# First two weight tiles of the dense part prepared inside the S5 output stage of a two-block layer kernel

## The chip, the cores and the metric

The kernel runs on one core of a Trainium2 chip. The metric is the device time of one execution in microseconds (us); lower is better. The engines are named as the profile names them: PE is the matrix engine (PEld its weight loads), DVE the vector engine, ACT the scalar engine, POOL the GpSimd engine, and SP the sync engine, which here only issues DMAs. A suffix q (SPq, PEq) means the sequencer of that engine.

## The reference, cut to what matters

One sequence of 2048 tokens by 1024 features goes through two blocks. The first block is a state-space mixer (S5) with a gated linear unit, a squared-ReLU feed-forward part and a gated per-layer embedding; the second has attention, an mLSTM and a convolution branch. The change touches the seam between the S5 mixer and everything behind it:

```python
y = (einsum('blgp,ghp->blgh', xs_re, c_re) - einsum('blgp,ghp->blgh', xs_im, c_im))
y = gelu(y.reshape(bsz, seqlen, D_MODEL) + d_skip * uf)      # S5 output
a, g = jnp.split(y @ w_glu, 2, axis=-1)                      # first weights of the dense part
mix = a * jax.nn.sigmoid(g)
x = x + mix
x = x + sqrelu_mlp(rmsnorm(x, norm_ffn), mlp_w1, mlp_w2)
```

Products are in float32 accuracy. The kernel gets that from three passes on a faster number format: each operand is split in a high part (a cast) and a low part (operand minus high part), and high x high, high x low and low x high are added up.

## The kernel before, in words

The program is a sequence of stages, each a `Block` in which every engine has its own instruction list; between two stages all engines meet at a barrier. The stages that matter here:

- `s5_states` (ends at about 214 us of the span): the scan over chunks.
- `s5_outputs` (214.5 to 332.7 us): eight rounds q = 0 to 7. In a round PE forms the S5 outputs of four pairs (L616 to L624), ACT applies the GELU (L653), PE turns the result (transposes, L635), ACT casts the first half of the tokens to the high part `AHL[:, 0, q]` (L660), DVE forms the low part `AHL[:, 1, q]` (L677) and copies the second half of the tokens to `later` (L681), and SP stores that to memory (L600, `y_hi`). PE and ACT turn and copy round q-1 behind the outputs of round q. SP also loads the matrices `s5_mt` of round q+2 (L442, eight DMAs of 128 KB for each round, each of many small pieces), in the same instruction list and so behind its wait for round q-1's store. DVE forms the matrices `ca` (L453 to L461). POOL has nothing to do in this stage.
- `dense` (from 332.7 us on): all the matrix products of the layer with streamed weights, for two halves of the tokens (`NB` = 2, `TB` = 1024). The weights are 124 tiles of 128 x 1024 floats, `wall`. Tile w goes through slot s = w % 2: SP loads it to `WR[s]` (`load`, L872, 512 KB), ACT casts it to `WH[s]` (`hi`, L910), POOL forms `WL[s]` (`lo`, L1129) and so frees `WR[s]` (semaphore `raw_free`), and PE multiplies (`product`, L1417). SP's order at the stage's start: `gains`, `w_gi`, four small vectors, tiles 0 and 1, tiles 2 and 3 (each behind `raw_free`), then `X`. ACT's order: the cast of `gwr` (L916), then tiles 0 and 1. POOL's order: `ones` (L1121), `gwl` (L1125), then tiles 0 and 1. PE starts on tile 0 when `raw_free` has reached 3, that is when `WL[0]` is there.

The steps of the prediction name: `s5_outputs` with its sync, scalar, vector and tensor programs; `s5_stage`, which opens the buffers; and in `dense` the first lines of the sync, scalar and gpsimd programs.

Of the kernel before, what the change touches and what calls it, by code (L numbers as in the profile page):

```python
# [11 lines left out]
P = 128  # L12
# [558 lines left out]
def s5_outputs(nc, env, d, ctx):  # L571

    sb, ps, sem = tools(nc, ctx)
    U, AHL, xs, ident = env["U"], env["AHL"], env["xs"], env["ident"]

    mt = [env["mt0"], sb("s5_mt1", [P, 2 * QP, T * H])]
    ca = [env["ca0"], sb("s5_ca1", [P, 2, QP, T, H])]
    yc = sb("s5_yc", [P, 2, T, P])
    later = sb("s5_later", [P, 2, SEQ // 2])
    by_step = lambda v: v.rearrange("p (c t) -> p t c", t=T)  # L580
    psy = [ps(f"s5_psy{i}", [P, 2, T * H]) for i in range(4)]
    psq = [ps(f"s5_psq{i}", [P, 4, NCH]) for i in range(4)]
    ld_m = [sem("s5_ld_m0"), sem("s5_ld_m1")]
    feed, fed = sem("s5_feed2"), sem("s5_fed2")
    y_mm, gelu_done, y_turned, hi_done, lo_done = (sem("s5_" + x) for x in ("y_mm", "gelu_done", "y_turned", "hi_done", "lo_done"))
    st_y = [sem("s5_st_y0"), sem("s5_st_y1")]
    with nc.Block() as block:
        @block.sync
        def _(sp):
            def load(q):  # L590
                if q >= 2:
                    sp.wait_ge(y_mm, 2 * (q - 1))
                s5_load(sp, d, q, mt[q % 2], ld_m[q % 2])

            load(1)
            for q in range(NQ):
                if q + 2 < NQ:
                    load(q + 2)
                sp.wait_ge(lo_done, 4 * (q + 1))
                sp.dma_start(d["y_hi"][q, :, SEQ // 2:], later[:, q % 2]).then_inc(st_y[q % 2], 16)  # L600
            for i in range(2):
                sp.wait_ge(st_y[i], 16 * (NQ // 2))

        @block.tensor
        def _(pe):
            def outputs(q):
                if q:
                    pe.wait_ge(ld_m[q % 2], 16 * S8 * ((q + 1) // 2))
                for pr in range(2):
                    if q:  # L610
                        pe.wait_ge(gelu_done, 4 * (q - 1) + 2 * pr + 2)
                    for jj in (2 * pr, 2 * pr + 1):
                        j = q * QP + jj
                        for g in range(2):
                            o, m = psy[2 * pr + g][:, jj % 2], mt[q % 2][:, 2 * jj + g]
                            pe.matmul(o, U[:, 0, 2 * j + g], m, start=True, stop=False)  # L616
                            pe.matmul(o[:, T * H // 2:], U[:, 1, 2 * j + g], m[:, 0:T * H // 2], start=False, stop=False)

                        if q:
                            pe.wait_ge(fed, q)  # L620
                        for ri in range(2):
                            for g in range(2):
                                rows = slice(g * 64, (g + 1) * 64)
                                last = pe.matmul(psy[2 * pr + g][:, jj % 2], xs[rows, ri, j, 0:NCH],  # L624
                                                 ca[q % 2][rows, ri, jj].rearrange("p t h -> p (t h)"),
                                                 start=False, stop=(ri == 1))
                    last.then_inc(y_mm, 1)

            def turn(q):
                pe.wait_ge(gelu_done, 4 * (q + 1))  # L630
                for i in range(4):
                    if q:
                        pe.wait_ge(lo_done, 4 * (q - 1) + i + 1)
                    for t in range(4):
                        last = pe.transpose(psq[i][:, t], yc[:, q % 2, 4 * i + t], ident[:])  # L635
                    last.then_inc(y_turned, 1)

            for q in range(NQ + 1):
                if q < NQ:
                    outputs(q)  # L640
                if q:
                    turn(q - 1)

        @block.scalar
        def _(act):
            for q in range(NQ + 1):
                if q < NQ:
                    for pr in range(2):
                        act.wait_ge(y_mm, 2 * q + pr + 1)
                        if q >= 2:  # L650
                            act.wait_ge(y_turned, 4 * (q - 1))
                        for g in range(2):
                            act.activation(yc[:, q % 2].rearrange("p t (j g h) -> p j g t h", h=H, g=2)[:, 2 * pr:2 * pr + 2, g],  # L653
                                           psy[2 * pr + g][:].rearrange("p j (t h) -> p j t h", h=H),
                                           ACT.Gelu_apprx_tanh).then_inc(gelu_done, 1)
                if q:
                    r = q - 1
                    for i in range(4):
                        act.wait_ge(y_turned, 4 * r + i + 1)
                        act.copy(by_step(AHL[:, 0, r])[:, 4 * i:4 * i + 4], psq[i][:, :, 0:NCH // 2]).then_inc(hi_done, 1)  # L660

        @block.vector
        def _(dve):
            def feedout(q):
                if q >= 2:
                    dve.wait_ge(y_mm, 2 * (q - 1))
                s5_feedout(dve, env, q, ca[q % 2], env["cat"], feed, N_FEED * (q - 1)).then_inc(fed, 1)
                dve.wait_ge(fed, q)

            feedout(1)  # L670
            for q in range(NQ):
                if q + 2 < NQ:
                    feedout(q + 2)
                for i in range(4):
                    dve.wait_ge(hi_done, 4 * q + i + 1)
                    steps = slice(4 * i, 4 * i + 4)
                    dve.tensor_tensor(by_step(AHL[:, 1, q])[:, steps], psq[i][:, :, 0:NCH // 2],  # L677
                                      by_step(AHL[:, 0, q])[:, steps].bitcast(F32), ALU.subtract)
                    if q >= 2:
                        dve.wait_ge(st_y[q % 2], 16 * (q // 2))  # L680
                    dve.tensor_copy(by_step(later[:, q % 2])[:, steps], psq[i][:, :, NCH // 2:]).then_inc(lo_done, 1)  # L681
# [20 lines left out]
def s5_stage(nc, env, d):  # L702
    with ExitStack() as stage:
# [6 lines left out]
        with ExitStack() as win:  # L710
            env["Win"] = win.enter_context(nc.sbuf_tensor("s5_Win", [P, NP, 2, 2, P], F32, side="right"))
            with ExitStack() as ctx:
                s5_setup(nc, env, d, ctx)
            env["xs"] = stage.enter_context(nc.sbuf_tensor("s5_xs", [P, 2, NP, NCH + 1], F32))
            env["mt0"] = stage.enter_context(nc.sbuf_tensor("s5_mt0", [P, 2 * QP, T * H], F32))
            env["ca0"] = stage.enter_context(nc.sbuf_tensor("s5_ca0", [P, 2, QP, T, H], F32))
            env["cat"] = stage.enter_context(nc.sbuf_tensor("s5_cat", [P, 2, QP, T, H], F32))
            with ExitStack() as ctx:
                s5_states(nc, env, d, ctx)
        with ExitStack() as ctx:  # L720
            s5_outputs(nc, env, d, ctx)

# [74 lines left out]

def dense(nc, env, d, ctx):
    ctx.callback(env["held"].close)
    sb, ps, sem = tools(nc, ctx)  # L800
    ident, eps = env["ident"], env["eps"]
    halves = lambda v: v.rearrange("p (a b) -> p a b", a=2)
# [5 lines left out]
    FH, FL = sb("FH", [P, F_TILES, TB], F32R), sb("FL", [P, F_TILES, TB], F32R)  # L808
    YR = nc.alloc_sbuf_tensor_at("YR", [P, KD, TB], F32, offset=nc.sbuf_base - 2 * F_TILES * TB * 4)
    SQ0 = nc.alloc_sbuf_tensor_at("SQ0", [P, 2, TB], F32, offset=nc.sbuf_base - 2 * F_TILES * TB * 4)  # L810
    WR = [sb(f"WR{i}", [P, TB]) for i in range(2)]
    WH = [sb(f"WH{i}", [P, TB], F32R) for i in range(2)]
    WL = [sb(f"WL{i}", [P, TB], F32R) for i in range(2)]
    SG = [sb(f"SG{i}", [P, 2, TB // 2]) for i in range(2)]
    V = [sb(f"V{i}", [P, 2, TB // 2]) for i in range(2)]
    RB = sb("RB", [P, TB])
# [43 lines left out]
    with nc.Block() as block:  # L860
        @block.sync
        def _(sp):
# [5 lines left out]
            def load(w, tile, s, n):  # L868
                free, at = (w + 1, tile) if n == 0 else (sp.snap(w + 1), sp.snap(tile, min_val=0, max_val=N_TILE - 1))
                sp.wait_ge(raw_free, free)  # L870
                tile = bass.ds(at, 1)
                sp.dma_start(WR[s][:], d["wall"][tile].rearrange("o p n -> p (o n)")).then_inc(raw_loaded[s], 16)  # L872

            for s in range(2):
                load(s, s, s, 0)
            for tb in range(NB):
                tok = tb * TB
                for s in range(2):
# [22 lines left out]
        def _(act):  # L901
# [12 lines left out]

            act.wait_ge(ld_g, 32)
            act.copy(gwh[:], gwr[:]).then_inc(gh_done, 1)  # L916
            for s in range(2):
                whi(0, s)
            for tb in range(NB):
                job0, w0 = tb * N_JOB, tb * (N_TILE // 2)  # L920

# [198 lines left out]
        def _(pool):  # L1120
# [10 lines left out]
            def wlo(w, s):  # L1131
                lo(w, s, WL[s][:], WH[s][:], WR[s][:])

            for s in range(2):
                wlo(s, s)
            for tb in range(NB):
                w0 = tb * N_TILE

# [1537 lines left out]
```

## Time and profile before

| what | value |
|---|---|
| three runs of the kernel, median (lowest to highest) | 3664.12 us (3663.32 to 3665.87) |
| the profiled execution's own time | 3664.25 us |
| its span, first to last instruction | 3662.6 us |
| outside the span | 1.65 us |
| PE busy, share of the span | 93% |
| DVE, ACT, POOL busy | 44%, 24%, 34% |
| mean granted TensorE clock | 0.971 of full speed |

How to read it: times in the trace count from the span's start. A line of a timeline gives start, length, engine, source line, operation, output and inputs, how many instructions were merged, and in brackets the idle time before it with what ended that idle time. The span is one profiled execution; the three runs are others. A granted clock of 1.00 is 2.4 GHz, 0.50 is 1.2 GHz.

### The profile page before, as it was taken

The numbers are of one execution on the slowest core, as the hardware profiler recorded it, in microseconds if no ns is written. First come the engines' busy times: TensorE is split into PE (matmuls) and PEld (weight loads), VectorE is DVE, ScalarE is ACT, GpSimd is POOL, SyncE is SP. The second block draws the span as 40 slices with busy tenths as digits, with TensorE's granted clock in tenths as the row PEclk, the third lists the DMA queues.
The fourth block names the chain that finished last, engine by engine and source line by source line (L and its number), as shares of the span: only waits on it lengthen the run. The fifth ranks groups of instructions, "written<-read, shape, count | busy, mean of one in ns | idle before, by whom it ended". The sixth has DMA issues, their size and how long they took to land. (4 is left out here: it accounts for less than half of the span.)

```text
span 3662.6 us, 42523 instructions
## 1 busy us (share of the span) xinstructions
PE 3414.0 (93%) x16929; PEld 2789.7 (76%) x16929; DVE 1618.2 (44%) x1643; ACT 883.3 (24%) x1323; POOL 1252.3 (34%) x710
## 2 busy tenths in 40 slices
PE   5467999999999999999999999999999999698899
PEld 5445878888888778888887888888777888476687
DVE  8774243333333556960133333333546971354411
ACT  4112131111111442112222111111342111466400
POOL 6800243333333532232325333333623231143521
PEclk8779999999999999999999999999999999899899
DMA  3135111111111103233311111111112231425553
GB/s 118 18 64 133 52 40 52 52 46 47 50 46 52 63 29 121 104 104 113 118 52 41 52 46 50 47 46 52 64 40 98 101 118 53 168 62 186 164 144 111
DMA packets 151459, 285.28 MB, mean 78 GB/s; under 512 B 16128, under 2 KB 91136, under 8 KB 149920
## 3 DMA queue, kind: packets, MB, share of 16 engines
q1 hardware_dynamic: 135200, 241.37, 21.8%
q10 hardware_dynamic: 16128, 42.08, 3.0%
q8 instruction: 92, 1.51, 0.2%
q14 instruction: 39, 0.32, 0.0%
HBM read 218.86 MB, written 64.55 MB: 77 GB/s over the span
## 5 line engine op out<-in xcount | busy, mean ns | idle before, releaser
L1417 PE MATMUL ps_job<-AHL,WH 128*128 128x512 f32 x4480 | 1382.6, 390 | 20.4 <-POOL WL L1129 18.9
L1129 POOL TENSOR_TENSOR WL<-WR,WH 128x1024 fp32r<-128x1024 f32 x216 | 524.4, 2428 | 1520.4 <-ACT WH L910 1520.4
L1417 PEld LDWEIGHTS ps_job<-AHL,WH 128*128 128x128 f32 x4480 | 841.7, 188 | 197.3 <-issue 19.1
L1417 PE MATMUL ps_job<-AHL,WL 128*128 128x512 f32 x2240 | 872.9, 390 | 0.0
L910 ACT CAST WH<-WR 128x1024 fp32r<-128x1024 f32 x216 | 227.5, 1054 | 1594.4 <-PE ps_job L1417 1445.3
L1417 PEld LDWEIGHTS ps_job<-AHL,WL 128*128 128x128 f32 x2240 | 421.2, 188 | 87.2
L1300 DVE TENSOR_TENSOR X<-X,ps_job 128x1024 f32<-128x1024 f32 x128 | 156.1, 1220 | 435.0 <-PE ps_job L1417 354.4
L1417 PE MATMUL ps_job<-FL,WH 128*128 128x512 f32 x768 | 299.1, 389 | 0.0
L1417 PE MATMUL ps_job<-FH,WH 128*128 128x512 f32 x768 | 299.1, 389 | 0.0
L1417 PE MATMUL ps_job<-FH,WL 128*128 128x512 f32 x768 | 299.1, 389 | 0.0
L1290 DVE SCALAR_TENSOR_TENSOR SG<-ps_job,RB 128x1024 f32<-128x1024 f32 x64 | 78.4, 1225 | 451.2 <-PE ps_job L1417 430.7
L1294 DVE TENSOR_TENSOR V<-SG 128x1024 f32<-128x1024 f32 x64 | 206.1, 3220 | 2.2
L1220 DVE TENSOR_TENSOR V<-ps_job,SG 128x1024 f32<-128x1024 f32 x32 | 39.1, 1223 | 367.9 <-PE ps_job L1417 246.2
L1354 DVE SCALAR_TENSOR_TENSOR CV<-CU,d_cw,CV 128x1024 f32<-128x1024 f32 x120 | 197.7, 1694 | 0.0
L1159 POOL TENSOR_TENSOR FL<-V,FH 128x1024 fp32r<-128x1024 f32 x64 | 153.1, 2392 | 76.0 <-DVE V L1294 76.0
L1417 PEld LDWEIGHTS ps_job<-FL,WH 128*128 128x128 f32 x768 | 144.3, 188 | 29.8
L1417 PEld LDWEIGHTS ps_job<-FH,WL 128*128 128x128 f32 x768 | 144.3, 188 | 29.8
L1417 PEld LDWEIGHTS ps_job<-FH,WH 128*128 128x128 f32 x768 | 144.3, 188 | 29.8
L1417 PE MATMUL ps_job<-TH,AHL 128*128 128x512 f32 x512 | 157.8, 390 | 0.0
L1142 POOL TENSOR_TENSOR AHL<-Tt,AHL 128x1024 fp32r<-128x1024 f32 x48 | 138.1, 2896 | 23.5 <-DVE Tt L1247 14.8
L1417 PE MATMUL ps_job<-FH,AHL 128*128 128x256 f32 (+1 forms) x512 | 125.0, 336 | 0.0
L616 PE MATMUL s_psy<-s_mt,s_U 128*128 128x256 f32 x128 | 43.7, 426 | 77.6 <-PEq L29 69.9
(408 smaller groups left out, 4900.4 us busy)
## 6 DMA issues: line engine op xcount, KB each, us to landing
WR<-in_wall SPq DMA_DIRECT2D x248, 512.0 KB, 3.5
fm_scratch<-V ACTq DMA_DIRECT2D x32, 512.0 KB
tm_scratch<-V ACTq DMA_DIRECT2D x28, 512.0 KB
s_U<-in_x_group SPq DMA_DIRECT2D x8, 1024.0 KB, 14.4
s_mt<-z_scratch SPq DMA_DIRECT2D x64, 128.0 KB, 5.1
X<-in_x_feat SPq DMA_DIRECT2D x2, 4096.0 KB, 15.2
m_oz<-tm_scratch SPq DMA_DIRECT2D x8, 1024.0 KB, 8.5
o_x<-x_scratch SPq DMA_DIRECT2D x16, 512.0 KB, 5.6
```

The source lines that it names most:

```text
L616: pe.matmul(o, U[:, 0, 2 * j + g], m, start=True, stop=False)
L910: act.copy(dst, WR[s][:]).then_inc(hi_done, 1)
L1129: pool.tensor_tensor(dst, raw, src.bitcast(F32), ALU.subtract).then_inc(raw_free, 1)
L1142: pool.tensor_tensor(AL[:, k], gained_at(i, k), AH[:, k].bitcast(F32), ALU.subtract).then_inc(al_done, 1)
L1159: pool.tensor_tensor(halves(FL[:, f]), V[f % 2][:], halves(FH[:, f]).bitcast(F32), ALU.subtract).then_inc(fl_done, 1)
L1220: dve.tensor_tensor(V[s][:], ps4[(job + 2 * s + 1) % 4][:], SG[s][:], ALU.mult).then_inc(mix_done, 1)
L1290: dve.scalar_tensor_tensor(SG[f % 2][:], ps4[(JOB_MLP + f) % 4][:], 0.0, halves(RB[:]), ALU.max, ALU.mult).then_inc(relu_done, 1)
L1294: dve.tensor_tensor(V[f % 2][:], SG[f % 2][:], SG[f % 2][:], ALU.mult).then_inc(v_done, 1)
L1300: dve.tensor_tensor(xm, xm, ps4[(JOB_MLP + F_TILES + m) % 4][:], ALU.add).then_inc(xadd, 1)
L1354: step = dve.scalar_tensor_tensor(CV[:, t], xk, c_w[:, t, k:k + 1], CV[:, t], ALU.mult, ALU.add)
L1417: last = pe.matmul(out, l, r, start=(k == 0 and i == 0), stop=(k == k_tiles - 1 and i == 2))
```

## The change

The buffers `WR`, `WH` and `WL` (two each) are no longer opened in `dense` but before `s5_outputs`, on the right side of the memory, and are closed with `dense`. In `s5_outputs` three things are added: SP issues the loads of weight tiles 0 and 1 in round q = 4, behind the loads of `s5_mt` for round 6; ACT casts both tiles in the last round, behind the GELUs of q = 7 and ahead of the casts of round 6; and POOL subtracts, which makes `WL`. In `dense` the loads, casts and subtractions of these two tiles are replaced by semaphore increments.

```diff
@@ s5_outputs @@
+    WR, WH, WL = env["WR"], env["WH"], env["WL"]
+    ld_w, wh_done, wl_done = [sem("s5_ld_w0"), sem("s5_ld_w1")], sem("s5_wh_done"), sem("s5_wl_done")
     with nc.Block() as block:
+        @block.gpsimd
+        def _(pool):
+            for s in range(2):
+                pool.wait_ge(wh_done, s + 1)
+                pool.tensor_tensor(WL[s][:], WR[s][:], WH[s][:].bitcast(F32), ALU.subtract).then_inc(wl_done, 1)
+            pool.wait_ge(wl_done, 2)
...
             for q in range(NQ):
                 if q + 2 < NQ:
                     load(q + 2)
+                if q == NQ // 2:
+                    for s in range(2):
+                        sp.dma_start(WR[s][:], d["wall"][s]).then_inc(ld_w[s], 16)
                 sp.wait_ge(lo_done, 4 * (q + 1))
...
                                            ACT.Gelu_apprx_tanh).then_inc(gelu_done, 1)
+                if q == NQ - 1:
+                    for s in range(2):
+                        act.wait_ge(ld_w[s], 16)
+                        act.copy(WH[s][:], WR[s][:]).then_inc(wh_done, 1)
                 if q:
@@ s5_stage @@
+        env["first"] = ExitStack()
+        for name, dt in (("WR", F32), ("WH", F32R), ("WL", F32R)):
+            env[name] = [env["first"].enter_context(nc.sbuf_tensor(f"{name}{i}", [P, TB], dt, side="right")) for i in range(2)]
@@ dense @@
+    ctx.callback(env["first"].close)
...
-    WR = [sb(f"WR{i}", [P, TB]) for i in range(2)]
-    WH = [sb(f"WH{i}", [P, TB], F32R) for i in range(2)]
-    WL = [sb(f"WL{i}", [P, TB], F32R) for i in range(2)]
+    WR, WH, WL = env["WR"], env["WH"], env["WL"]
...                                                            # SP
             for s in range(2):
-                load(s, s, s, 0)
+                sp.sem_inc(raw_loaded[s], 16)
...                                                            # ACT
-            for s in range(2):
-                whi(0, s)
+            act.sem_inc(hi_done, 2)
...                                                            # POOL
-            for s in range(2):
-                wlo(s, s)
+            pool.sem_inc(raw_free, 2)
```

## Rows read from the trace of the kernel before

**Rows 1.** The page, part 1: busy time, share of the span and instructions.
```profile
PE 3414.0 (93%) x16929; PEld 2789.7 (76%) x16929; DVE 1618.2 (44%) x1643; ACT 883.3 (24%) x1323; POOL 1252.3 (34%) x710
```

**Rows 2.** Busy time by stretch: stretch, length, engines' busy time (count), PE clock, DMA share, GB/s.
```profile
332.70:343.40 10.70, 0.01 (x1) 0.04 (x1) 0.46 (x6) 2.33 (x3) 3.14 (x4) 0.50 0.36 108
343.40:347.00 3.60, 3.60 (x9) 2.92 (x10) 0.00 (x0) 0.00 (x0) 2.05 (x1) 0.53 0.56 156
```

**Rows 3.** Timeline of the dense part's first 11 us.
```profile
332.71 0.33 SPq L863 DMA_DIRECT2D gains<-in_gains  x1
...
334.91 0.24 ACT L916 CAST gwh<-gwr 128x64 fp32r<-128x64 f32 x1 [8.00 <-DMA gwr<-in_w_gi]
335.23 0.32 POOL L1125 TENSOR_TENSOR gwl<-gwr,gwh 128x64 fp32r<-128x64 f32 x1 [2.31 <-ACT gwh L916]
335.46 0.91 SPq L872 DMA_DIRECT2D WR<-in_wall  x2
...
339.66 1.04 ACT L910 CAST WH<-WR 128x1024 fp32r<-128x1024 f32 x1 [4.51 <-DMA WR<-in_wall]
340.88 1.04 ACT L910 CAST WH<-WR 128x1024 fp32r<-128x1024 f32 x1 [0.17 <-DMA WR<-in_wall]
340.79 4.66 POOL L1129 TENSOR_TENSOR WL<-WR,WH 128x1024 fp32r<-128x1024 f32 x2 [5.24 <-ACT WH L910]
343.39 1.19 PE L1417 MATMUL ps_job<-AHL,WH 128*128 128x512 f32 x2 [17.11 <-POOL WL L1129]
```

**Rows 4.** Line L1129 from 335 to 420 us: min/median/max duration in ns.
```profile
L1129 POOL TENSOR_TENSOR WL<-WR,WH x8: 2344/2389/2398, 340.8 to 412.5; 128x1024 fp32r<-128x1024 f32 x8
```

**Rows 5.** Timeline of DVE and SP at the end of the S5 output stage.
```profile
321.73 0.62 DVE L677 TENSOR_TENSOR AHL<-s_psq,AHL 128x256 fp32r<-128x256 f32 x1 [10.65 <-ACT AHL L660]
...
328.57 0.57 DVE L681 COPY s_later<-s_psq 128x256 f32<-128x256 f32 x1
...
329.17 0.32 SPq L600 DMA_DIRECT2D y_hi_scratch<-s_later  x1
```

**Rows 6.** Timeline of ACT: the last round of S5, and a cast behind another instruction.
```profile
320.13 1.09 ACT L653 ACTIVATE s_yc<-s_psy 128x512 f32<-128x512 f32 x2 [4.05 <-PE s_psy L624]
321.10 1.88 ACT L660 CAST AHL<-s_psq 128x256 fp32r<-128x256 f32 x4
323.65 0.59 ACT L660 CAST AHL<-s_psq 128x256 fp32r<-128x256 f32 x1 [0.67 <-PE s_psq L635]
...
362.99 1.03 ACT L928 ACTIVATE SG<-ps_job 128x1024 f32<-128x1024 f32 x1
363.92 1.04 ACT L910 CAST WH<-WR 128x1024 fp32r<-128x1024 f32 x1
```

**Rows 7.** Timeline of SP: DMA issues around the place of the new loads.
```profile
284.56 4.18 SPq L442 DMA_DIRECT2D s_mt<-z_scratch  x8
298.78 0.34 SPq L600 DMA_DIRECT2D y_hi_scratch<-s_later  x1
299.16 4.15 SPq L442 DMA_DIRECT2D s_mt<-z_scratch  x8
```

**Rows 8.** Busy time by stretch, columns as in rows 2: DMA traffic there.
```profile
288.00:294.00 6.00, 6.00 (x42) 4.79 (x41) 3.20 (x3) 1.81 (x4) 0.00 (x0) 1.00 1.09 134
294.00:298.00 4.00, 3.91 (x28) 3.07 (x27) 3.05 (x7) 2.14 (x5) 0.00 (x0) 1.00 0.00 0
```

**Rows 9.** Timeline of PE and its weight loads: rounds 3, 6 and 7 begin.
```profile
254.78 1.22 PE L616 MATMUL s_psy<-s_mt,s_U 128*128 128x256 f32 x2 [2.94 <-DMA s_mt<-z_scratch]
...
295.21 0.30 PEld L616 LDWEIGHTS s_psy<-s_mt,s_U 128*128 128x128 f32 x2 [0.33 <-DMA s_mt<-z_scratch]
...
309.74 0.70 PE L616 MATMUL s_psy<-s_mt,s_U 128*128 128x256 f32 x2 [2.28 <-DMA s_mt<-z_scratch]
```

**Rows 10.** PE's stretches: length, busy, granted clock, DMA share, GB/s.
```profile
254.70:258.00 3.30, 3.22 (x10) 0.50 0.56 172
309.70:313.00 3.30, 3.26 (x20) 1.00 0.34 135
```

**Rows 11.** DVE's groups by form, 330 to 2000 us: busy us, mean ns, idle before.
```profile
L1294 DVE TENSOR_TENSOR V<-SG 128x1024 f32<-128x1024 f32 x36 | 115.5, 3207 | 1.2
L1300 DVE TENSOR_TENSOR X<-X,ps_job 128x1024 f32<-128x1024 f32 x70 | 85.4, 1220 | 239.4 <-PE ps_job L1417 194.1 <-PE ps_job L1434 44.2
```

**Rows 12.** Timeline of DVE: its first use of the dense part's products.
```profile
367.25 1.22 DVE L1220 TENSOR_TENSOR V<-ps_job,SG 128x1024 f32<-128x1024 f32 x1 [30.22 <-PE ps_job L1417]
```

## The prediction

> **What bounds the kernel now.** I read first the page's busy shares: PE is busy for 3414.0 of 3662.6 us [rows 1], so the kernel as a whole is a row of products on PE, and what can be won without changing the products lies in the stretches where PE stands still. The busy times by stretch show one of them at the seam that the change touches: in 332.7 to 343.4 us, the first 10.7 us of the dense part, PE does nothing [rows 2]. The timeline of that stretch [rows 3] says why, read from its last row backwards. PE's first product at 343.39 ends an idle time of 17.11 us that is put down to POOL's `WL`. POOL began that subtraction at 340.79, when ACT's cast was there; the cast waited for the load of `WR` until 339.66; and the load was issued at 335.46, because SP puts six small loads ahead of it. So the chain at the seam is stage start, small loads, tile load (4.2 us), cast (1.04), subtraction, product. Nothing else that PE needs lies in it. The other side of the seam is the end of the S5 stage: DVE works without a gap from 321.73 to 328.57 + 0.57 = 329.14, sixteen instructions (L677 and L681 in turn, eight times; the first and the last stand in [rows 5]), SP stores behind the last one at 329.17, and the stage's end waits for that store; the dense part begins at 332.71.
>
> **What is taken away.** In the dense part `raw_free` now reaches 4 by an increment that stands behind POOL's `gwl`. `gwl` starts at 335.23 and takes 0.32, so it ends at 335.55 [rows 3]. It hangs on the loads of `gains` and `gwr` (ACT's cast at 334.91 waited for them), and these stay. The step from POOL's end to PE's start I take from the same view: the first subtraction starts at 340.79 and takes between 2.34 and 2.40 [rows 4], I take 2.35, so it ends at 343.14, and PE starts at 343.39, 0.25 later. PE would start at 335.55 + 0.25 = 335.80 in the old frame. Gain: 343.39 - 335.80 = **7.59 us**. Two loads, two casts and two subtractions go from the dense part; of their time only what lay in this chain counts. What is late next is `gwr`. The other things PE waits for at the start are increments and memsets at the head of each engine's list and do not wait for a load of a tile.
>
> Behind the start the order stays. SP's loads of tiles 2 and 3 and of `X` no longer wait for the splits of tiles 0 and 1, so they come earlier against PE than before. That is worth nothing: DVE's first use of the products and of `X` waited for PE, 30.22 us, and not for the load of `X` [rows 12]. The ACT casts of tiles 2 and 3 wait for PE to be done with `WH`, so they move with PE. From there on all goes on as before, only earlier, and the gain arrives at the end in full.
>
> **What is added: ACT.** Two casts of 128x1024 go between the last GELUs and the casts of `AHL` of round 6. The `AHL` casts began at 321.10, straight behind the GELUs, and not because they waited for PE [rows 6]. A cast of this form behind another ACT instruction takes 1.04 us from start to end, but the distance from one start to the next is 363.92 - 362.99 = 0.93 [rows 6]. Two of them: 1.86 (2.08 if nothing overlaps). Who waits for that: DVE's first L677 of the tail was released by exactly this `AHL` cast (10.65 us idle, then 321.73), and from there DVE is without a gap, so the whole tail, the last store and the stage's end move by the same time. PE's turns of round 7 and ACT's casts of round 7 follow DVE's tail and have slack: the cast that begins at 323.65 ends at 324.24 [rows 6], and DVE comes to its result only behind eight instructions, at about 321.73 + 7.41 / 2 = 325.4, half of the tail [rows 5]. Cost: **1.86 us**, on the path.
>
> **POOL.** The two subtractions, at 2.39 each [rows 4], start when the first cast is there, about 322.2, and end at about 327.1. The tail on DVE then ends at 329.14 + 1.86 = 331.0. So they are hidden by DVE's tail; without that cover they would cost up to 4.8. The remaining question is whether they slow DVE, with which they now run at the same time. The nearest rows: with POOL's subtractions running all the time in the dense part, DVE's L1294, which reads memory operands alone, takes 3207 ns, while L1300 of the same size, which reads one operand from PSUM, takes 1220 [rows 11]. L677 and L681 both read PSUM (`psq`), so they are like L1300: I take 0. The far end is that every one of the two subtractions blocks DVE once for its length, 2 x 2.39 = 4.8.
>
> The Trainium skill has the mechanism (SBUF — State Buffer, section SBUF: two separate sides): GpSimd and a vector instruction with two SBUF inputs, or in a 2-port mode, hold a shared port pair in turn, and the loser is blocked for the whole instruction. By that rule a vector instruction with a PSUM input isn't touched and the term is 0; the overview's shorter wording, that the interface is shared, would give the far end. The two rows agree with the rule as it stands, and so that far end gets a small chance below.
>
> **SP.** Two loads of 512 KB are issued behind the eight loads of `s5_mt` for round 6, which were issued from 284.56 on for 4.18 us [rows 7]; so at about 288.8 and 289.2. SP then waits for round 4's store in any case (298.78), so its own issue time costs nothing. The DMA traffic of the round's loads goes on until about 294, and from 294 to 298 it is zero [rows 8]. PE took up round 6 at 295.21 with 0.33 us of waiting for `s5_mt` [rows 9]. If the new loads go behind the older ones, they fill the empty 294 to 298.8: the same 1 MB took from 335.46 to 340.88 in the dense part [rows 3], 5.4 us with its latency. Then the cost is 0, and I take that. If they share the engines with the last loads of `s5_mt` all along, these come later by at most 340.88 - 335.46 less the latency, some 3.3; round 7 waited 2.28 us for its own `s5_mt` [rows 9], whose load hangs on round 4's store and doesn't move, so 2.28 of that is given back: at most +1.0.
>
> The Trainium skill (DMA: Bandwidth & Descriptors, section Queues, rings and completion order) says that descriptors of one issuing engine are consumed in ring order, though they may finish out of it. By that the term would be 0 and not +1.0. No row here shows two such loads crossing.
>
> **The clock.** PE's first 3.6 us of the dense part ran at a granted clock of 0.53 (half of 2.4 GHz) [rows 2], after 17.11 us without work. After the change the idle time is 17.11 - 7.59 = 9.5. A pause of 2.94 us was already followed by a stretch at 0.50, one of 2.28 was not [rows 9, 10], so 9.5 will be: no change. Bounds: half of the 3.6 us stretch, 1.8 us, would be won if the clock stayed up; the same is lost if the slow stretch at the new place is twice as long. I keep both ends for the range.
>
> **The sum.** 3664.25 (profiled execution) - 7.59 + 1.86 = 3658.52. The three runs have their median 0.13 below the profiled execution, which is within their spread of 2.6, so I give **3658.5 us**, 5.7 us or 0.15% less. About 0.2% (7.3 us) is what a measurement of this kernel can tell from no change, so the likeliest answer by that bound is "same", though on the faster side of it.
>
> **The rivals.**
> (a) The slow stretch of the clock or the casts come out better: with the clock held up, 3658.5 - 1.8 = 3656.7. For it: the pause at the seam is nearly halved. Against: [rows 9, 10].
> (b) The slow stretch is longer: 3660.3. For it: where it begins and ends differs from place to place. Against: nothing but the one row.
> (c) The loads of the tiles hold up round 6's `s5_mt`: 3659.5.
> (d) POOL blocks DVE in the tail: 3658.5 + 4.8 = 3663.3; the change then gives almost nothing. Against: L1300.
> (e) Slower than before. Place: the DMA engines between 294 and 304. The `s5_mt` loads move 1 MB in about 294 - 284.56 = 9.4 us; if the new loads went at that rate, they would last until about 303.4 instead of leaving the engines free at 298.78, and round 7's `s5_mt` would land 4.6 us later. PE's pause there would be 2.28 + 4.6 = 6.9, above the 2.94 behind which the clock fell, and 3.3 us at half clock cost 1.65 more. Together -7.59 + 1.86 + 4.6 + 1.65 = +0.5: 3664.8. It decides from a transfer time of about 8.9 us on; the same loads in the dense part took 5.4, which speaks against it.
> (f) The change doesn't do what it says: PE's start is held by another wait that the long wait for `WL` hid. Each microsecond of it takes one from the gain; what I see in the stretch are memsets and small loads, with SP's last small load issued before 335.46 [rows 3]; a wait of 1 us there would give 3659.5.
>
> **Chances and range.** Forecast 0.60, with its own range 3657.0 to 3660.0 from the runs' spread; (a) 0.12; (b) 0.10; (c) 0.06; (d) 0.05; (e) 0.03; (f) 0.04. For 8 in 10 the range takes in the forecast, most of (a), (b) and (c): 3655.9 to 3661.6. Faster by over 0.2% means below 3656.8: about half of (a) and the lower tail of the forecast, a share of one in five of it, together 0.18. Slower by over 0.2% needs more than (e) gives: 0.02. Within 0.2%: 0.80.
>
> **What would show it.** In the profile after: PE's pause at the seam about 9.5 us, since its last product of the S5 stage moves with DVE's tail, and ended by `gwl` or an increment of POOL and no longer by `WL`; from SP's `gains` to PE's first product 3.1 us instead of 10.7; DVE's tail starting 1.9 us later against the last GELU, with means of 0.58 us for L677 and L681 as before; POOL's subtractions over before DVE's tail is; round 7's wait for `s5_mt` still about 2.3. Wrong would be: DVE instructions of over 2 us in the tail (d), a wait above 3 us for `s5_mt` (c, e), or another releaser of PE at the start (f).

## The result, and the profile after

The changed kernel takes 3724.44 us (median of 5 runs, 3723.23 to 3729.63) against 3663.32 for the kernel before in the same series: ratio 1.0169, 95% interval 1.0156 to 1.0182. It is 61 us slower, where 5.7 us faster was forecast. The profiled execution took 3729.63 us, with a span of 3727.9; it is the slowest of the five, so the spans below differ by 65.3 us where the medians differ by 61.

| | before | after |
|---|---|---|
| span of the profiled execution | 3662.6 | 3727.9 |
| dense part begins (SP's `gains`) | 332.71 | 333.31 |
| PE's first product of the dense part | 343.39 | 336.07 |
| start of PE's last `TH,AHL` product, the end of the dense part within 0.7 us | 3133.3 | 3196.1 |
| from there to the span's end | 529.3 | 531.8 |
| PE busy | 3414.0 | 3487.8 |

The table says where the time went. The first product comes 7.3 us earlier, so the seam gained. (Where the first product lies differs from execution to execution: 341.8 to 343.7 in the profiles of the kernel before and the three experiments that keep its seam, 332.0 to 337.0 in those of the changed kernel and the fourteen that have the new one.) Then the dense part, which began earlier, ends 62.8 us later: it lasts 2860.0 us instead of 2789.9 from first to last product. The rest differs by 2.5. Together: -7.3 + 70.1 + 2.5 = 65.3, the difference of the spans.

The seam first, in the timelines of the changed kernel (ACT, DVE, SP, POOL, PE; lines L671 and L594 are the new casts and subtractions), to be held against [rows 3, 5, 6]:

```profile
318.82 1.08 ACT L665 ACTIVATE s_yc<-s_psy 128x512 f32<-128x512 f32 x2 [4.05 <-PE s_psy L636]
319.79 1.99 ACT L671 CAST WH<-WR 128x1024 fp32r<-128x1024 f32 x2
321.67 1.89 ACT L676 CAST AHL<-s_psq 128x256 fp32r<-128x256 f32 x4
...
322.30 0.59 DVE L693 TENSOR_TENSOR AHL<-s_psq,AHL 128x256 fp32r<-128x256 f32 x1 [11.63 <-ACT AHL L676]
...
329.17 0.57 DVE L697 COPY s_later<-s_psq 128x256 f32<-128x256 f32 x1
...
333.31 0.33 SPq L881 DMA_DIRECT2D gains<-in_gains  x1
...
320.92 4.69 POOL L594 TENSOR_TENSOR WL<-WR,WH 128x1024 fp32r<-128x1024 f32 x2 [129.84 <-ACT WH L671]
...
335.84 0.32 POOL L1142 TENSOR_TENSOR gwl<-gwr,gwh 128x64 fp32r<-128x64 f32 x1 [2.32 <-ACT gwh L934]
...
336.07 1.19 PE L1433 MATMUL ps_job<-AHL,WH 128*128 128x512 f32 x2 [8.83 <-POOLq L1151]
```

PE is released by POOL's sequencer (the increment at L1151) and no longer by `WL`. This is the forecast picture. What nobody had put in the sum stands in the rows of the product line, of the kernel before (L1417) and after (L1433); the three numbers behind the count are the shortest, median and longest duration in ns:

```profile
L1417 PE MATMUL ps_job<-AHL,WH x4480: 387/390/767, 343.4 to 2966.9; 128*128 128x512 f32 x195
L1417 PE MATMUL ps_job<-FH,WH x768: 388/389/390, 583.5 to 2619.2; 128*128 128x512 f32 x192
L1417 PE MATMUL ps_job<-TH,AHL x512: 388/389/398, 1607.3 to 3133.3; 128*128 128x512 f32 x171
```

```profile
L1433 PE MATMUL ps_job<-AHL,WH x4480: 389/396/767, 336.1 to 3029.7; 128*128 128x512 f32 x195
L1433 PE MATMUL ps_job<-FH,WH x768: 394/396/397, 582.5 to 2673.8; 128*128 128x512 f32 x192
L1433 PE MATMUL ps_job<-TH,AHL x512: 388/389/397, 1637.2 to 3196.1; 128*128 128x512 f32 x171
```

The products that have `WH` or `WL` as weights went from a median of 389 or 390 to 396 ns (one group of 128 from 393); the products with `AHL` as weights (the row of `TH,AHL`) did not. The clock was the same and PE was busy without a gap, as 100 us of the feed-forward part show, first before, then after (stretch, length, busy with count, granted clock, DMA share, GB/s):

```profile
900.00:1000.00 100.00, 100.00 (x443) 1.00 0.15 47
```

```profile
900.00:1000.00 100.00, 100.00 (x431) 1.00 0.16 47
```

443 products in the stretch became 431. With `WH` or `WL` as weights there are 4480 + 2240 + 2304 at the main product line and 768 + 384 + 192 at others, 10,368 in all: 70.1 us over 10,368 is 6.8 ns for each, the step from 389 to 396.

### The profile page after: what moved, and what is told of

Read it like the earlier page. It is cut to its first block and busy times, and to the rows that moved or that the text cites. A ratio compares the mean times of both kernels' runs of the same rounds, so it can differ in the third digit from the quotient of the medians.

```text
span 3727.9 us, 42528 instructions
## 1 busy us (share of the span) xinstructions
PE 3487.8 (94%) x16929; PEld 2795.7 (75%) x16929; DVE 1622.9 (44%) x1643; ACT 882.3 (24%) x1323; POOL 1249.8 (34%) x710
## 5 line engine op out<-in xcount | busy, mean ns | idle before, releaser
L1433 PE MATMUL ps_job<-AHL,WH 128*128 128x512 f32 x4480 | 1412.4, 396 | 14.8 <-POOLq L1151 8.8
L1433 PEld LDWEIGHTS ps_job<-AHL,WH 128*128 128x128 f32 x4480 | 843.1, 188 | 221.2 <-issue 10.9
L1433 PE MATMUL ps_job<-AHL,WL 128*128 128x512 f32 x2240 | 887.5, 396 | 0.0
L1433 PEld LDWEIGHTS ps_job<-AHL,WL 128*128 128x128 f32 x2240 | 421.9, 188 | 101.9
L1433 PE MATMUL ps_job<-FH,WL 128*128 128x512 f32 x768 | 303.9, 396 | 0.0
L1433 PE MATMUL ps_job<-FL,WH 128*128 128x512 f32 x768 | 303.8, 396 | 0.0
L1433 PE MATMUL ps_job<-FH,WH 128*128 128x512 f32 x768 | 303.8, 396 | 0.0
L1433 PEld LDWEIGHTS ps_job<-FL,WH 128*128 128x128 f32 x768 | 144.4, 188 | 34.9
L1433 PEld LDWEIGHTS ps_job<-FH,WL 128*128 128x128 f32 x768 | 144.3, 188 | 34.9
L1433 PEld LDWEIGHTS ps_job<-FH,WH 128*128 128x128 f32 x768 | 144.3, 188 | 34.8
L1433 PE MATMUL ps_job<-TH,AHL 128*128 128x512 f32 x512 | 157.7, 389 | 0.0
L1433 PE MATMUL ps_job<-FH,AHL 128*128 128x256 f32 (+1 forms) x512 | 125.0, 336 | 0.0
```

The source lines that it names most:

```text
L1433: last = pe.matmul(out, l, r, start=(k == 0 and i == 0), stop=(k == k_tiles - 1 and i == 2))
```

## The experiments

Three theories for the 6.8 ns were stated first: the start addresses (A), the region at the right end of the memory (B), and the changed overlap of the engines' work (C). The allocator gives the addresses: `WH0` lay at byte 189120 of a partition before the change and lies at 217056 after it, `AHL` at 17088 in both. In the table at the end of this section the distance is the address of the weights minus that of the moving operand, modulo 256.

**e1_aligned.** One line in `s5_stage`, behind `env["first"] = ExitStack()`:

```diff
+        env["first"].enter_context(nc.sbuf_tensor("pad_r", [P, 8], F32, side="right"))
```

> The changed kernel with one edit: 32 bytes are left free at the right end of the memory before the six weight buffers are placed, so every one of them starts at a multiple of 64 bytes (WH0 at 217024) instead of 32 bytes beside one (217056). Theory A (PE takes longer for products whose weights start 32 bytes off a multiple of 64): the 61 us are gone and only the seam is left, 3664 - 5.7 = 3658 us, products with WH and WL again at a median of 389 to 390 ns instead of 396. Theory B (the region at the right end of the memory is slower for PE's reads, whatever the alignment): no change against the changed kernel, 3724 us, 396 ns. Theory C (the moved loads, casts and splits shift the overlap so that PE is slowed all along): 3724 us, 396 ns.

Measured: 3657.31 us, ratio 0.9981 (0.9972 to 0.9991); `AHL,WH` and `AHL,WL` at 389. 32 bytes take the whole loss away. B and C fall.

**e2_place_only.** The kernel before, with the six buffers opened as in the change and nothing moved in time.

> The kernel before with the six weight buffers placed on the right side exactly as in the changed kernel (WH0 at 217056), while loads, casts and splits of tiles 0 and 1 stay in the dense part. Theories A and B: PE's 10,368 products with WH or WL as weights are 6.8 ns slower each, 70 us in all, and no seam gain: 3734 us. Theory C: 3664 us.

Measured: 3731.35 us, ratio 1.0181 (1.0164 to 1.0198), `AHL,WH` at 396.

**e3_shift32_left.** The kernel before, `WH` and `WL` in the old place and order, 32 bytes on:

```diff
+    sb("pad_a", [P, 8])
     WH = [sb(f"WH{i}", [P, TB], F32R) for i in range(2)]
     WL = [sb(f"WL{i}", [P, TB], F32R) for i in range(2)]
+    sb("pad_b", [P, 8])
```

> The kernel before with 32 free bytes ahead of WH0 (and 32 behind WL1), so WH and WL stay in the middle of the memory in their old order but start 32 bytes off a multiple of 64 (WH0 at 189152 instead of 189120); nothing is moved in time. Theory A: 3734 us, 396 ns for each product with WH or WL. Theory B and theory C: 3664 us, 390 ns.

Measured: 3731.12 us, ratio 1.0180 (1.0163 to 1.0197), 396 ns. A shift of 32 bytes in the middle of the memory, with nothing moved in time, makes the 66 us (the buffers behind `WL` shift too, by 64 bytes, but PE reads none of them in the products whose time changed). This is the cleanest run against B and C.

**e4_wl_only.** e1_aligned, with a second pad of 32 bytes between `WH1` and `WL0`.

> The kernel of e1_aligned with WL0 and WL1 alone shifted to 32 bytes off a multiple of 64 (WH stays aligned). Theory A, in its form that each load of weights pays by itself: only the 3456 products with WL as weights pay, 3456 x 6.8 ns = 23 us, so 3681 us, and the rows of the products with WH keep 390 ns. If instead it is the relation between two weight buffers that counts (WH against WL), all products change or none: 3658 or 3724 us. Theory B: 3724 us.

Measured: 3705.70 us, ratio 1.0107 (1.0090 to 1.0124): 48 us above e1_aligned, twice what I expected. The rows show how:

```profile
L1436 PE MATMUL ps_job<-FH,WH x768: 389/389/389, 581.3 to 2654.9; 128*128 128x512 f32 x192
L1436 PE MATMUL ps_job<-FL,WH x768: 392/392/392, 581.5 to 2655.1; 128*128 128x512 f32 x192
L1436 PE MATMUL ps_job<-FH,WL x768: 397/398/398, 581.8 to 2655.4; 128*128 128x512 f32 x192
```

The three stand in PE's order. The product ahead of a product with `WL`, `FL,WH`, also grows by 3 ns, and that with `WL` by 9, so a price per load of weights is too simple. Measured from start to start, the steps behind `FH,WH`, `FL,WH` and `FH,WL` have means of 228.3, 229.2 and 235.8 ns in this trace, and 226.6 to 226.7 in the kernel before. That is 13.3 ns for each product with `WL`, and 3456 of them make 46 of the 48 us.

Two pairs of operands could matter: a product's own weights and moving operand, or the moving operand that streams now and the weights that are loaded for the next product. While `FH,WL` streams, `WH` is loaded, at distance 0 from `FH`, and still this step has the most, 9.1 ns; while `FL,WH` streams, `WL` is loaded, at distance 224, and this step has 2.5. So by the recorded starts most of the cost goes with the product's own pair. Why the two other steps grow is not shown.

**e5_moving.** e1_aligned with `sb("pad_c", [P, 8])` behind `ident` near the left end, so the moving operands shift by 32 bytes.

> e1_aligned with 32 bytes added near the left end of the memory, so that AHL, FH, FL and TH, TL start 32 bytes off a multiple of 64 (AHL at 17120 instead of 17088), while WH and WL stay aligned. In most products of the dense part these are the moving operands, in 1536 products at its end AHL is the weights. If an unaligned moving operand costs as much as unaligned weights: about 10,400 x 6.8 ns + 10 us more, 3657 + 80 = 3737 us, and products of AHL with WH at 396 ns. If only the load of weights pays: 1536 x 6.8 ns = 10 us more, 3668 us, products with WH at 389 and those with AHL as weights at 396.

Measured: 3721.38 us, ratio 1.0157 (1.0141 to 1.0174), and a row that neither reading had in it:

```profile
L1435 PE MATMUL ps_job<-AHL,WH x4480: 389/395/763, 337.0 to 3026.3; 128*128 128x512 f32 x195
L1435 PE MATMUL ps_job<-TH,AHL x512: 388/389/398, 1635.3 to 3192.7; 128*128 128x512 f32 x171
```

`TH` and `AHL` are both shifted and their product stays at 389. So it isn't alignment of one operand that costs. A new theory: the distance between the two operands of a product counts. In this kernel it is 224 for `AHL,WH` and 0 for `TH,AHL`.

**e6_a128.** e1_aligned with 96 instead of 32 free bytes.

> e1_aligned with 96 instead of 32 free bytes at the right end, so WH and WL start at a multiple of 128 bytes (WH0 at 216960) instead of 64 beside one. If the grain is 64 bytes: no change, 3657 us, 389 ns. If it is 128 bytes, the aligned kernel still pays and this one gains as much again: about 3657 - 70 = 3587 us, 383 ns.

Measured: 3680.11 us, ratio 1.0042 (1.0027 to 1.0056): 23 us slower than e1_aligned, so `WH` at a multiple of 128 is worse, and theory A in its first form is gone. Here products at one distance (192) differ among themselves: `FH,WH`, `FL,WH` and `FH,WL` have medians of 392, 394 and 388 ns.

**e9_both32.** The changed kernel with `pad_c` alone; `WH0` is at 217056 as in the change, `AHL` at 17120.

> The changed kernel with nothing aligned on the right side (WH0 at 217056, as in the change), but with 32 bytes added near the left end, so AHL, FH, FL start at 96 modulo 128 bytes too (AHL at 17120). Weights and moving operand are both 32 off a multiple of 64, and their distance is a multiple of 128. Relation theory (what costs is the distance between the weights' and the moving operand's address modulo 128, not where each starts): products of AHL with WH at 389 ns, and the last projection, whose operands now also match, 5 us shorter: 3652 us. Absolute theory (each operand pays by itself for a start off a multiple of 64, as e1 and e5 alone would let one think): 3657 + 66 + 64 = 3787 us, 400 ns or more.

Measured: 3657.02 us, ratio 0.9983 (0.9974 to 0.9992):

```profile
L1434 PE MATMUL ps_job<-AHL,WH x4480: 387/389/763, 335.5 to 2962.7; 128*128 128x512 f32 x195
L1434 PE MATMUL ps_job<-FH,WH x768: 389/389/389, 576.4 to 2614.9; 128*128 128x512 f32 x192
```

Both operands are 32 bytes off a multiple of 64, and the products are fast. The distance decides. The time is 5 us above my sum: the last projection did gain 4.4 us (193.9 to 189.5), the dense part lasted 3.6 us longer than in e1_aligned, and I have no row for that. The dense parts of the seven kernels at distance 0 lie between 2789.8 and 2793.6 us (table below), so 4 us there is what one profile can tell from another.

**e10_both64, e11_p160.** e6_a128 with `AHL` moved by 64 bytes too; the change with 160 free bytes.

> The kernel of e6_a128 (WH0 at 216960, 0 modulo 128; 23 us slower than e1_aligned) with AHL, FH, FL moved by 64 bytes as well (AHL at 17152, 0 modulo 128). Relation theory: the distance is a multiple of 128 again, 389 ns, 3657 us. Absolute theory (a start at 0 modulo 128 is the worse one): 3680 us or more.

> The changed kernel with 160 free bytes at the right end: WH0 at 216896, 64 modulo 128 and 64 modulo 256, while AHL stays at 192 modulo 256. If the distance counts modulo 128: as e1_aligned, 3657 us, 389 ns. If it counts modulo 256 or more: slower than that, by the 23 us of e6_a128 or more.

Measured: 3717.16 us, ratio 1.0149 (1.0133 to 1.0164), and 3718.14 us, ratio 1.0153 (1.0138 to 1.0169). Both expectations of a modulus of 128 fell, and in the same way: in both kernels the distance is 128 modulo 256, and the dense part lasted 2849.2 and 2847.7 us. The modulus isn't 128. It isn't 512 for distance 0 either, since the kernel before has 0 modulo 512 and e1_aligned 256 modulo 512, with 2789.9 and 2790.0 us.

**e13_d64, e14_d96, e15_d160.** e12_best (below) with 224, 192 and 128 free bytes.

> The kernel of e12_best (3652 us, distance 0 modulo 256 between weights and moving operand) with 224 instead of 32 free bytes, so the distance is 64 (WH0 at 216832). Two readings. Distance 0 is where the two streams of PE get in each other's way least, and everything else costs: between the 23 us of distance 192 and the 65 of 32 more, 3675 to 3717 us. Or each distance has its own value and 0 isn't the best: below 3652, at the lowest 3652 - 110 = 3542 us, were a product of 512 columns to follow the last after 216 ns instead of 227.

> As e13_d64 with 192 free bytes: distance 96 (WH0 at 216864). First reading: 3675 to 3717 us, nearer to the upper end since 96 is, as 32 is, no multiple of 64. Second reading: anything from 3542 us.

> As e13_d64 with 128 free bytes: distance 160 (WH0 at 216928). First reading: 3675 to 3717 us. Second reading: anything from 3542 us.

Measured (two runs each): 3718.18, 3731.95 and 3720.55 us, ratios 1.0147, 1.0185 and 1.0154. No distance beats 0, so the first reading holds in its sign, but all three lie above its range of 3675 to 3717 us, by 1, 15 and 4 us. Of the distances in steps of 32 bytes, all but 0 cost between 23 and 80 us. At 160 the groups of one kernel again differ: `AHL,WL` has a median of 399 ns, `AHL,WH` 394 and `FL,WH` 393.

**e17_fh_only.** e1_aligned with `sb("pad_x", [P, 8])` ahead of `X` in `dense`: `FH`, `FL`, `TH` move by 32 bytes, `AHL`, `WH`, `WL` stay. Two kinds of products with the same weights in one kernel.

> e1_aligned with 32 bytes in front of X in the dense part, so that X, Tt (with TH, TL), FH and FL move by 32 bytes while AHL, WH and WL stay. The products of the feed-forward part's second half (3072 with FH or FL as moving operand) then have distance 224 modulo 256 to their weights, all with AHL as moving operand stay at 0. If the pair of one product counts: AHL with WH or WL stays at 389 ns, FH and FL with WH or WL go to 394 to 396, and TH with AHL as weights, which stayed at 389 in every kernel so far, goes to 394 to 396 for the first time; 3072 x 6.6 = 20 us and up to 10 us for the 1536 with AHL as weights: 3677 to 3687 us. If it is the place of WH and WL against something else: all products with WH and WL change alike, and TH with AHL stays at 389.

Measured: 3687.64 us, ratio 1.0068 (1.0051 to 1.0085).

```profile
L1435 PE MATMUL ps_job<-AHL,WH x4480: 387/389/763, 334.2 to 2983.0; 128*128 128x512 f32 x195
L1435 PE MATMUL ps_job<-AHL,WL x2240: 388/389/628, 335.2 to 2983.3; 128*128 128x512 f32 x187
L1435 PE MATMUL ps_job<-FH,WH x768: 393/395/397, 575.0 to 2635.0; 128*128 128x512 f32 x192
L1435 PE MATMUL ps_job<-TH,AHL x512: 393/395/397, 1608.8 to 3152.6; 128*128 128x512 f32 x171
```

With `WH` as weights, `AHL` is fast and `FH` is slow in the same run, and `TH,AHL` is slow for the first time, in the only kernel in which its own two operands changed their distance. So it is neither the weights' place nor the moving operand's place alone. In these stretches the neighbouring products have the same distance too, so this run doesn't part a product's own pair from the pair of present moving operand and next weights; for that there is only e4_wl_only. The time is 0.6 us above the expected range.

**e16_before_ow, e7_ow.** The kernel before, and e1_aligned, each with one line that brings the last projection's weights to distance 0:

```diff
+            held.enter_context(nc.sbuf_tensor("pad_o", [P, 8], F32, side="right"))
             for name in ("cv_acc", "cv_z"):
```

> e1_aligned with a second pad of 32 bytes at the right end of the stages behind the dense part. It brings the weights of the last projection, o_wh and o_wl, to a multiple of 64 bytes (o_wh at 196544 instead of 196576); they were 32 off it in the kernel before as well, whose rows for L2544 have medians of 394 to 396 ns against 389 to 390 in the dense part. Alignment theory: these 768 products lose 6.5 ns each, 5.0 us in all, 3657.3 - 5.0 = 3652 us, medians 389 to 390. If that line is slower for another reason: 3657 us and 394 to 396 ns.

> The kernel before with one line added, 32 free bytes at the right end of the stages behind the dense part, so that o_wh and o_wl lie at distance 0 modulo 256 from the moving operand o_mh instead of 224; nothing of the change is in it. Distance theory: 768 products 6.5 ns faster, 5.0 us, 3659 us, medians of the last projection's products 389 instead of 394 to 396 ns. If the effect needs something of the change: 3664 us.

The text on record for e16 gives 224 as the old distance; worked out again from the addresses (196576 - 17088, since `o_mh` lies where `AHL` lay) it is 32. Measured: e7_ow 3651.78 us, ratio 0.9970 (0.9958 to 0.9981); e16_before_ow 3659.58 us, ratio 0.9987 (0.9977 to 0.9997), 5.3 us by the medians where 5.0 was expected. The row of the kernel before, then that of e16:

```profile
L2544 PE MATMUL o_y_ps<-o_wh,o_mh x256: 392/396/796, 3462.5 to 3655.9; 128*128 128x512 f32 x128
```

```profile
L2544 PE MATMUL o_y_ps<-o_wh,o_mh x256: 387/389/792, 3462.9 to 3652.1; 128*128 128x512 f32 x128
```

So the effect is in the kernel before too, with nothing of the change in it.

**e8_early, e12_best.** The casts between the GELU pairs of the last round instead of behind them; e12 joins e7 and e8.

```diff
                                            ACT.Gelu_apprx_tanh).then_inc(gelu_done, 1)
-                if q == NQ - 1:
-                    for s in range(2):
-                        act.wait_ge(ld_w[s], 16)
-                        act.copy(WH[s][:], WR[s][:]).then_inc(wh_done, 1)
+                        if q == NQ - 1 and pr == 0:
+                            for s in range(2):
+                                act.wait_ge(ld_w[s], 16)
+                                act.copy(WH[s][:], WR[s][:]).then_inc(wh_done, 1)
```

> e1_aligned with the two casts of the last S5 round put between the GELUs of its first and its second pair, where ACT stood idle for 4.05 us, instead of behind both. My account of the seam: the 1.9 us by which the casts delayed DVE's tail go, 3657.3 - 1.9 = 3655.4 us; the first L677-type instruction of the tail starts 0.6 us behind the last GELU pair as in the kernel before. Rival (the tail waited for something else, such as POOL's splits): 3657 us.

> e1_aligned with both remedies, the weights of the last projection aligned (e7_ow) and the casts between the GELU pairs (e8_early). Sum: 3657.3 - 5.5 (e7) - 0.9 (e8) = 3651 us by what the two did alone; by the seam account alone (1.9 us for the casts) 3650 us.

Measured: e8 3656.37 us, ratio 0.9979 (0.9969 to 0.9988); e12 3652.18 us, ratio 0.9970 (0.9958 to 0.9983). In the trace of e8 the account holds:

```profile
315.79 1.08 ACT L665 ACTIVATE s_yc<-s_psy 128x512 f32<-128x512 f32 x2 [6.74 <-PE s_psy L636]
316.76 1.99 ACT L671 CAST WH<-WR 128x1024 fp32r<-128x1024 f32 x2
320.93 1.09 ACT L665 ACTIVATE s_yc<-s_psy 128x512 f32<-128x512 f32 x2 [2.18 <-PE s_psy L636]
...
322.55 0.62 DVE L693 TENSOR_TENSOR AHL<-s_psq,AHL 128x256 fp32r<-128x256 f32 x1 [10.93 <-ACT AHL L676]
```

From the last GELU pair to DVE's tail it is 1.62 us, as in the kernel before (1.60), and not 3.48. In the medians the 1.9 us don't show (e8 is 0.9 us below e1, e12 is 0.4 above e7, while the runs of one kernel are 5 to 8 us apart), so the gain of the earlier casts is seen in the trace alone. e7_ow and e12_best are the fastest kernels of the study, both 0.3% below the kernel before.

| distance | kernel | dense part, first product to last `TH,AHL`, us | more than at 0 |
|---|---|---|---|
| 0 | before; e1; e7; e8; e9; e12; e16 | 2789.9; 2790.0; 2790.2; 2790.2; 2793.6; 2792.2; 2789.8 | |
| 32 | after; e2; e3 | 2860.0; 2858.0; 2856.3 | 66 to 70 |
| 64 | e13 | 2857.7 | 68 |
| 96 | e14 | 2869.5 | 80 |
| 128 | e10; e11 | 2849.2; 2847.7 | 58 to 59 |
| 160 | e15 | 2859.9 | 70 |
| 192 | e6 | 2813.5 | 24 |
| 224 | e5 | 2855.7 | 66 |

## Why the prediction was wrong, by its own steps

**What is taken away: right.** From SP's `gains` to PE's first product it was 10.68 us and is 336.07 - 333.31 = 2.76: 7.92 gained for 7.59 forecast. The 0.33 between them is the end of `gwl`: the increment behind it released PE at 336.07, ahead of `gwl`'s own end at 335.84 + 0.32 = 336.16.

**ACT: right.** From the last GELU pair's start to DVE's tail 1.60 us before, 322.30 - 318.82 = 3.48 after: 1.88 for 1.86. DVE's tail lasts 7.44 us for 7.41.

**POOL: right.** The subtractions end at 325.6, ahead of the tail's end at 329.7, and the tail's instructions keep 0.56 to 0.60 us. Rival (d) is out.

**SP: no cost that shows.** The waits for `s_mt` at rounds 6 and 7 in the changed kernel:

```profile
294.82 0.70 PE L628 MATMUL s_psy<-s_mt,s_U 128*128 128x256 f32 x2 [1.09 <-DMA s_mt<-z_scratch]
308.43 0.70 PE L628 MATMUL s_psy<-s_mt,s_U 128*128 128x256 f32 x2 [1.36 <-DMA s_mt<-z_scratch]
```

And in e2_place_only, which has none of the new loads in this stage:

```profile
294.86 0.70 PE L616 MATMUL s_psy<-s_mt,s_U 128*128 128x256 f32 x2 [0.96 <-DMA s_mt<-z_scratch]
308.69 0.70 PE L616 MATMUL s_psy<-s_mt,s_U 128*128 128x256 f32 x2 [1.59 <-DMA s_mt<-z_scratch]
```

Round 6 waits 1.09 us where [rows 9] show 0.33 before the weight load, and round 7 waits 1.36, where I had said it would stay at 2.3. Against the one profile of the kernel before, this looks like a crossing of the new loads with the older ones. But e2_place_only and e3_shift32_left wait 0.96 and 0.99 us at round 6, and 1.59 and 1.79 at round 7, without any new load. With the new loads, e1_aligned has 1.85 and 0.60. So the two waits differ by more than a microsecond from profile to profile, and rival (c) is neither seen nor excluded. For the same reason no run here agrees or disagrees with the ring order that the Trainium skill states (DMA: Bandwidth & Descriptors, section Queues, rings and completion order).

**The clock: right.** PE's pause at the seam was 8.83 us for 9.5 forecast. Then the granted clock was 0.50 from 336.1 to 340.3 and full from 341.0 on, some 4.2 us at half speed instead of 3.5, which is within the bounds of the range.

So the seam did about what was forecast: e1_aligned, which is the change with its 32 bytes, has 3657.31 us where its own series has 3665.16 for the kernel before, 7.9 us less (3 to 10 by the interval) where 5.7 was said.

**The step that failed** is the sentence "From there on all goes on as before, only earlier". Of the change's four parts three were priced and the fourth was not: the buffers' new place. I took placement to be free and gave it neither a term, nor bounds, nor a rival, and (e), the only case on the slower side, was about something else. The trace of before held the hint in one row, that of L2544 shown above: the last projection, the same shape and kind of product as L1417, with weights on the right side of the memory, took 396 ns against 390. It wasn't among the rows I read, since the change doesn't touch that line.

The runs put 6.8 ns for each of 10,368 products, 70 us, in the place of that missing term: the weights' distance from the moving operand went from 0 to 32 modulo 256.

The Trainium skill (SBUF — State Buffer, section SBUF: two separate sides) says of the engines' ports that PE never waits on anyone. The Trainium skill (TensorE: Matmul & The Clock Gate, section Step-by-step: what each phase is for) gives PE two independent read ports, one for the weights and one for the moving operand, and says that loading the next weights steals no read bandwidth from the running product. Neither place speaks of addresses, and a reader would take from them that the distance costs nothing. At another distance than 0, e3_shift32_left measures 7 ns and e17_fh_only 5 to 7 ns for each product, so the measurement decides.

**What stays open.** The runs show that the distance decides between fast and slow, not what in the memory does it. That the product's own pair counts more than the next weights rests on e4_wl_only alone. The order of the eight values (192 cheap, 96 dearest), the split in e4 and the differences between products at one distance (e6, e15) are not explained, distances finer than 32 bytes were not tried, and products of other shapes than 128 x 512 with 128 columns of weights were not measured.

## What to carry to other kernels

When a change moves a buffer that PE reads, work out the distance between the weights' and the moving operand's addresses modulo 256 bytes before and after, and price it by a row of the same product at that distance: here 7 ns for each of 10,368 products outweighed the microseconds won at a seam ten times over. A line of the same kind elsewhere in the kernel that takes a few ns more than its twin is worth a look, since one pad of 32 bytes may be its cure, as it was for the last projection here (5.3 us). An edit that "only changes where something lies" gets a term in the sum like any other.

## What the runs showed of the hardware that I had not expected

For products of 128 x 512 with 128 columns of weights in this kernel, the time of one depends on the distance of its two operands modulo 256 bytes: 389 ns at 0 and, by the medians of the rows, 396 at 32, 394 to 396 at 64 and 224, 397 at 96, 393 at 128, 393 to 399 at 160 and 388 to 394 at 192. The operands' own alignment did not matter (e9 at 32 off a multiple of 64, e1 on one, both 389). An increment that follows a GpSimd instruction in its list can be seen by PE before that instruction has ended: PE started 0.09 us ahead of the end of `gwl`, going by the trace, whose spans on POOL are rough. In all fifteen profiles that have this seam PE starts 0.23 to 0.26 us behind the start of `gwl`, whose own length is 0.32.
